# Eleven pages of the second sequence are issued by GpSimd at the end of the mLSTM stage

## The chip, the cores and the metric

The kernel runs on one core of one Trainium2 chip. The metric is the device time of one execution in microseconds, lower is better. The engines are TensorE (PE in the profile), its weight load (PEld), VectorE (DVE), ScalarE (ACT), GpSimd (POOL) and SyncE (SP). A "q" behind a name (POOLq) is that engine's sequencer.

## The reference

One decoder layer (DEPTH is 1) is computed for a prompt of 1024 tokens and for 8 sample sequences of 4 tokens with 4096 past tokens each. The mixer has an mLSTM branch and a sparse attention branch. For the change two parts matter:

```python
# mlstm_mixer: chunkwise recurrence, then per-head norm and output gate
h, C, n, m = mlstm_chunked(q, k, vh, i_pre, log_f, C0, n0, m0)
h = h * lax.rsqrt(jnp.mean(h * h, axis=-1, keepdims=True) + EPS) * p['m_norm']
h = jax.nn.sigmoid(og) * h.reshape(B, T, M_DIM)
# nsa_mixer: the past rows come through a page table; blocks of 32 rows are compressed
past = cache_nsa_kv[l][page_table].reshape(bs, past_len, 4, N_KV, N_HD)
blk = kb.reshape(B, nc, CMP_BLK, G, D) + pe[None, None, :, None, :]
flat = jnp.moveaxis(blk, 3, 2).reshape(B, nc, G, CMP_BLK * D)
kcmp = jax.nn.gelu(flat @ w1) @ w2        # and the same for the values
```

A sample sequence has 32 pages of 128 tokens. The compression reads the first two of the four parts of each page, which is 128 KB a page and 4 MB a sequence.

## The kernel before, in words

The kernel is a row of stages, each a block with one instruction stream per engine. The helper `stage` (line 135 on) opens and closes a stage: at its end every engine drains and all engines meet, and no engine starts on the next stage before the last of them has arrived. The profile puts these closing instructions (DRAIN, EVENT_SEMAPHORE) on line 146.

**The stage `mlstm` (line 515 on)** computes the prompt's mLSTM in 8 chunks of 128 tokens. Its streams are written out by hand. At its end PE turns the eight scaled output chunks (line 762), ACT copies them out of PSUM (line 816), and DVE closes with one memset that waits for all eight copies. GpSimd's last work there is the scaling of chunks 0 to 2 (line 628, `scale(i)`). SP meanwhile issues the 32 pages of the first sample sequence (sequence 0) into the buffer `first_pages` (line 565), in slots whose former content has been read by then, and then stores the prompt's final state (lines 598 to 600).

**The stage `sab` (`states_and_blocks`, line 1016 on)** computes the compressed blocks of the 8 sample sequences and their mLSTM step. The page buffers are two, used in turn: `first_pages` (called `kv`) and, right behind it, `sab_kv` (`kv1`); sequence n uses buffer n % 2. `load(eng, n, first, count, done)` (line 1088) reads page numbers from the table and issues one DMA a page (line 1093). For sequence 1, which goes into `sab_kv`, SP issues pages 0 to 15 and GpSimd pages 16 to 31, at the very start of the stage. For sequences 2 to 7, SP issues 12 pages, ACT 8 and GpSimd 12, and these wait until PE is through with both products of sequence n-2, the last user of the same buffer (`layer1_ready >= 2 * (n - 1)`). PE runs a fixed order: `queries_keys` (lines 1141 to 1144), `first(0, 0)`, `first(0, 1)`, two products on the prompt's own rows, `first(1, 0)`, `first(1, 1)`, and so on to `first(7, 1)`. `first(n, kv)` is the big product over the pages of sequence n (line 1001) and waits for their arrival.

In memory the second page buffer lies over tiles of the stage `mlstm`: its slots 0 to 15 (16 KB in each partition) over `kT`, which holds the numerators until the end of that stage, and slots 16 to 26 (11,264 bytes) over `xs`, `ys`, `mnorm`, `dec` and `kw` (11,648 bytes together).

Of the kernel before, what the change touches and what calls it, by code (L numbers as in the profile page):

```python
# [20 lines left out]
ds = bass.ds  # L21

P = 128
# [3 lines left out]
NTILE = TP // P  # L27
NSEQ, TS = 8, 4
# [12 lines left out]
PAST, PAGE = 4096, 128  # L41
NPAGE = PAST // PAGE
# [462 lines left out]


W1_AT = 221152


def heads_weights(ring):  # L510
# [4 lines left out]
def mlstm(nc, A, O, K, N, zm, zn, hm, cw, wqk, tokm, tokn, sm, pages, psum):  # L515
# [9 lines left out]
    with stage(nc, "mlstm") as (ctx, sem):  # L525
# [18 lines left out]
                 "ex_ready", "weights_ready", "mb_ready", "dec_ready", "exp_done", "score_ready", "weighted", "kw_ready", "update_ready",  # L544
                 "inter_ready", "intra_ready", "C_ready", "num_ready", "ss_ready", "tail", "square_ready", "root_ready",
                 "intra_copied", "gated", "factors_ready", "scaled", "scaled_pool", "scaled_act", "state_copied", "turned", "h_stored", "C_turned", "finished",
                 "stored")
        S = {n: sem(n) for n in names}
        block = ctx.enter_context(nc.Block())
        wide = lambda bank: psum[:, bank:bank + 2, :].rearrange("p b (h t) -> p (b h) t", h=2)[:, :, 0:MD + 1]  # L550
# [24 lines left out]
        def pages_over_queries(eng, some, done):  # L575
            page = page_numbers(nc, eng, pages, some[0], len(some), N["n_pool"])
            eng.wait_ge(S["inter_ready"], NTILE)
            for e, g in zip(some, page):
                first_page(eng, e, g, done)

        @block.sync
        def _(sp):
            sp.dma_start(xs[:, :, :, 0:3], A["m_state"]).then_inc(S["loaded"], 16)
            sp.dma_start(mnorm[:, :, :], A["m_norm"].partition_broadcast(P)).then_inc(S["loaded"], 16)
            sp.dma_start(O["p_mconv"], zm[:, :, TP - 3:TP]).then_inc(S["conv_kept"], 16)
            sp.dma_start(N["w1"][:, :, :, :], A["cmp_w1"]).then_inc(N["w1_ahead"], 16)
            sp.wait_ge(S["staged"], 4)
            sp.dma_start(O["s_mconv"], xs[:, :, :, TS:TS + 3]).then_inc(S["stored"], 16)
            sp.wait_ge(S["conv_kept"], 16)
            sp.dma_start(N["C"][:, :, :, :], A["s_C0"]).then_inc(N["C_ahead"], 16)  # L590
            sp.dma_start(O["zkv"], zn[:, 4:8, :]).then_inc(S["stored"], 16)
            sp.dma_start(O["tkv"], tokn[:, :, 0:2 * P]).then_inc(S["stored"], 16)
            sp.dma_start(O["winp"], A["winp"]).then_inc(S["stored"], 16)
            pages_over_keys(sp, N["kv_ahead"])
            pages_over_queries(sp, range(0, NPAGE // 2), N["kv_ahead"])
            sp.wait_ge(S["finished"], 1)
            sp.wait_ge(S["state_copied"], 1)
            sp.dma_start(O["p_C"], Ct[:, :, :]).then_inc(S["stored"], 16)
            sp.dma_start(O["p_n"], cn[:, :]).then_inc(S["stored"], 16)
            sp.dma_start(O["p_m"], mc[0:1, NTILE, :]).then_inc(S["stored"], 16)  # L600
            sp.wait_ge(S["stored"], 112)

        @block.gpsimd
        def _(pool):
            ones = tokm[:, 0:NTILE, C_V:C_V + MH * (MD + 1)].rearrange("p t (h v) -> p t h v", h=MH)[:, :, :, MD]
            nc.gpsimd.memset(ones, 1.0).then_inc(S["ones_set"], 1)
            pool.wait_ge(S["loaded"], 32)

            def weigh_keys(i):
                pool.wait_ge(S["weights_ready"], 1)  # L610
                pool.wait_ge(S["kt_copied"], 2 * MH)
                if i >= 2:
                    pool.wait_ge(S["update_ready"], i - 1)
                w = chunks(ex[:, WL, :])[:, i, :].unsqueeze(2).to_broadcast([P, MH, MD])
                nc.gpsimd.tensor_tensor(kw[:, i % 2, :, :], kt[:, i, :, :], w, ALU.mult).then_inc(S["kw_ready"], 1)

            def scale_output_gate(t):
                x = tokm[:, t, C_OG:C_OG + 512]
                nc.gpsimd.tensor_tensor(x, x, mnorm[:, :, :].rearrange("p h v -> p (h v)"), ALU.mult).then_inc(S["og_scaled"], 1)

            def gate(i):
                pool.wait_ge(S["og_scaled"], i + 1)
                pool.wait_ge(S["ss_ready"], i + 1)
                nc.gpsimd.tensor_tensor(chunk(num, i), chunk(num, i), tokm[:, i, C_OG:C_OG + 512].rearrange("p (h v) -> p h v", h=MH), ALU.mult
                                        ).then_inc(S["gated"], 1)

            def scale(i):
                nc.gpsimd.tensor_tensor(chunk(num, i), chunk(num, i), chunks(fac[:, :])[:, i, :].unsqueeze(2).to_broadcast([P, MH, MD]), ALU.mult
                                        ).then_inc(S["scaled_pool"], 1)

            weigh_keys(0)
            for i in range(1, NTILE):
                weigh_keys(i)
                scale_output_gate(i - 1)
                if i >= 3:
                    gate(i - 3)
            scale_output_gate(NTILE - 1)
            gate(NTILE - 3)
            gate(NTILE - 2)
            pool.wait_ge(S["factors_ready"], 1)  # L640
            for i in POOL_SCALES:
                pool.wait_ge(S["gated"], i + 1)
                scale(i)

        @block.tensor
        def _(pe):
# [369 lines left out]
def states_and_blocks(nc, A, O, K, N, zn, hm, tokm, sm, pages, ring, tile_at, spare, psum):  # L1016
# [7 lines left out]
    layer1_bank = lambda n, kv: 4 + kv if n == 1 else kv  # L1024
    with stage(nc, "sab") as (ctx, sem):
        assert nc.sbuf_base == N["kv_at"]
        top = N["kv_at"] + 4 * NPAGE * 2 * PAGE

        def sb(n, shape):
            nonlocal top  # L1030
# [1 line left out]
            top += -(-4 * int(np.prod(shape[1:])) // 32) * 32  # L1032
            return t

        kv_in = [N["kv"], sb("kv1", [P, NPAGE, 2 * PAGE])]
        NPR = TP // 2
        place, limit = spare

# [42 lines left out]
        per_head = lambda v, n: v.unsqueeze(2).to_broadcast([NS, MH, n])  # L1081
        per_all = lambda v: v.unsqueeze(1).to_broadcast([NS, MH, NS])
        SP_N, POOL_N, ACT_N = 12, 12, 8
        FIRST_SP = NPAGE // 2
        hard = lambda n: FIRST_SP if n == 1 else SP_N + ACT_N
        soft = lambda n: NPAGE - hard(n)

        def load(eng, n, first, count, done):
            page = page_numbers(nc, eng, pages, n * NPAGE + first, count, N["n_pool"])
# [14 lines left out]

        @block.sync
        def _(sp):
            load(sp, 1, 0, FIRST_SP, loaded)
            sp.dma_start(w2[:, :, :], A["cmp_w2"]).then_inc(S["w_loaded"], 16)
            sp.dma_start(rel[:, :], A["rel"]).then_inc(S["vec_loaded"], 16)
            sp.wait_ge(S["qk_ready"], 1)  # L1110
# [18 lines left out]

        @block.gpsimd  # L1130
        def _(pool):
            load(pool, 1, FIRST_SP, NPAGE - FIRST_SP, loaded_soft)
            for n in range(2, NSEQ):
                load(pool, n, SP_N + ACT_N, POOL_N, loaded_soft)

        @block.tensor
        def _(pe):
# [38 lines left out]
            def first(n, kv):  # L1176
# [3 lines left out]
                elif kv == 0:  # L1180
                    pe.wait_ge(loaded[n % 2], 16 * pages_before(n, hard))
                    pe.wait_ge(loaded_soft[n % 2], 16 * pages_before(n, soft))
                if n == 1 and kv == 0:
                    pe.wait_ge(S["qk_copied"], 3)
                elif n == 1:
                    pe.wait_ge(S["q_read"], 1)
                elif n == 2:
                    pe.wait_ge(S["act_ready"], kv + 1)
                elif n:
                    pe.wait_ge(S["act_ready"], 2 * (n - 1) + kv + 1)  # L1190
# [2560 lines left out]
def build(nc, A, O):  # L3751
    with ExitStack() as ctx:
# [20 lines left out]
        x = low  # L3773
# [15 lines left out]
        with ExitStack() as c:  # L3789
            N = {"n_pool": A["pool"].shape[0],  # L3790

                 "soft": {n: ctx.enter_context(nc.semaphore(n)) for n in ("c0", "c1", "n0", "n1")}}
            N.update({n: ctx.enter_context(nc.semaphore(n)) for n in ("w1_ahead", "C_ahead", "kv_ahead")})
            tile_at = lambda name, shape, at: nc.alloc_sbuf_tensor_at(name, shape, F32, offset=at)
            N.update(kv_at=nc.sbuf_base, kv=tile_at("first_pages", [P, NPAGE, 2 * PAGE], nc.sbuf_base),
                     w1=tile_at("block_w1", [P, 2, CB // 2, HD], W1_AT), C=tile_at("sample_C", [P, NSEQ, MH, MD], place["low"] + 4 * 4 * T))
            mlstm(nc, A, O, K, N, zm, zn, hm, cw, heads_weights(ring), tokm, tokn, sm, pages, psum)
            N.update(block_views(tile_at("blocks", [P, BLOCKS_W], place["tokm"])))
# [211 lines left out]
```

## Time and profile before

| | us |
|---|---|
| median of 3 runs | 2373.71 |
| lowest and highest of them | 2369.65, 2380.47 |
| the profiled execution, device time | 2377.2 |
| its span, first to last instruction | 2375.5 |
| PE busy in it | 2251.5 (95%) |
| GpSimd busy in it | 439.4 (18%) |
| granted TensorE clock, mean | 0.971 |

The span starts with the first instruction; all places in time below are microseconds from there. The stage `mlstm` ends at about 382.5 and the stage `sab` at about 498. A line of the profile names the engine, the source line, the operation, what is written and what is read, and the count; in brackets stands for how long the engine was idle before it and what released it.

### The profile page before, as it was taken

Reading aid. Unit: us, or ns where it says so; the run is one execution under the profiler, and the core shown is the slowest. Engines: PE = TensorE matmul, PEld = TensorE weight load, DVE = VectorE, ACT = ScalarE, POOL = GpSimd, SP = SyncE. Lnnn points to the kernel's source line nnn. Section 1 sums busy time; section 2 is a strip of 40 time slices with the busy share of each in tenths; the row PEclk is TensorE's granted clock in tenths of the full one; section 3 lists DMA queues with packets and bytes.
Section 4 is the critical chain, followed back from the end, with each engine's and each line's share of the span. In section 5 each row is a group of like instructions: output and inputs, shape, how many; then the busy total and the mean of one; then the engine's idle time right before and its main releaser. Section 6 shows DMA issues by size and latency. Waiting matters only on the chain. (4 is left out here: it accounts for less than half of the span.)

```text
span 2375.5 us, 39417 instructions
## 1 busy us (share of the span) xinstructions
PE 2251.5 (95%) x16031; PEld 2072.3 (87%) x16031; DVE 1083.8 (46%) x2432; ACT 719.8 (30%) x1444; POOL 439.4 (18%) x393
## 2 busy tenths in 40 slices
PE   8999998988988989999999999999999999999996
PEld 7799977856555689999999978999999999999995
DVE  2213354356666741222254346186545555542336
ACT  4221253135655630111342225352111111121123
POOL 0000035402223121121111100112222222122220
PEclk9999999879999999999999999999999999999998
DMA  4211097964434331210411444121111111111312
GB/s 146 97 49 46 27 187 242 308 224 124 144 126 150 115 113 41 69 43 27 153 36 45 160 173 162 43 91 63 45 45 45 46 53 45 35 43 47 118 41 82
DMA packets 114159, 228.71 MB, mean 96 GB/s; under 512 B 23394, under 2 KB 76291, under 8 KB 110588
## 3 DMA queue, kind: packets, MB, share of 16 engines
q1 hardware_dynamic: 91578, 182.12, 24.3%
q0 software_dynamic: 10368, 28.33, 3.6%
q10 hardware_dynamic: 12034, 15.76, 2.0%
q8 instruction: 127, 2.08, 0.4%
q14 instruction: 52, 0.43, 0.1%
HBM read 202.91 MB, written 27.45 MB: 97 GB/s over the span
## 5 line engine op out<-in xcount | busy, mean ns | idle before, releaser
L88 PE MATMUL psum<-x_half_high,ff_half 128*128 128x352 f32 x3240 | 789.4, 323 | 9.8 <-POOL ff_half L69 4.9
L88 PEld LDWEIGHTS psum<-x_half_high,ff_half 128*128 128x128 f32 x3240 | 566.3, 189 | 11.3 <-POOL ff_half L69 5.9
L88 PE MATMUL psum<-h_again_low,ff_half 128*128 128x352 f32 x1176 | 378.4, 322 | 0.0
L69 POOL TENSOR_TENSOR ff_half<-ring,ff_half 128x1024 fp32r<-128x1024 f32 (+2 forms) x85 | 177.4, 2087 | 751.2 <-ACT ff_half L3293 751.2
L88 PEld LDWEIGHTS psum<-h_again_low,ff_half 128*128 128x128 f32 x1176 | 222.2, 189 | 0.0
L3293 ACT ACTIVATE ff_half<-ring 128x1024 fp32r<-128x1024 f32 (+2 forms) x88 | 78.0, 888 | 428.7 <-PE psum L88 407.5
L88 PE MATMUL psum<-merged_high,oq_half 128*128 128x352 f32 x768 | 189.8, 327 | 9.3 <-DVE oq_half L69 7.7
L88 PE MATMUL psum<-mid_low,ff_half 128*128 128x352 f32 x516 | 166.3, 322 | 0.0
L88 PEld LDWEIGHTS psum<-merged_high,oq_half 128*128 128x128 f32 x768 | 136.1, 191 | 9.9 <-DVE oq_half L69 8.0
L88 PE MATMUL psum<-x_half_high,mg_w_high 128*128 128x352 f32 x384 | 124.0, 323 | 1.2 <-ACT gated L2317 1.2
L88 PE MATMUL psum<-h_again_low,mg_w_high 128*128 128x352 f32 x384 | 123.1, 321 | 0.0
L88 PE MATMUL psum<-x_half_high,mg_w_low 128*128 128x352 f32 x384 | 123.1, 320 | 0.0
L1945 ACT ACTIVATE na_pt<-psum 128x512 f32<-128x512 f32 (+1 forms) x170 | 86.4, 543 | 87.1 <-PE psum L1820 78.6
L1643 POOL DMA_DIRECT2D na_kv<-in_pool x128 | 69.2, 540 | 225.1 <-PE psum L1847 150.8
L1820 PEld LDWEIGHTS psum<-consts,na_p 128*128 128x128 f32 x528 | 57.8, 144 | 53.5 <-DVE na_p L2094 31.7
L3604 DVE TENSOR_TENSOR h_again<-h_again,psum 128x352 f32<-128x352 f32 x96 | 49.8, 520 | 117.3 <-PE psum L88 117.1
L88 PE MATMUL psum<-in_half,h_high 128*128 128x512 f32 (+3 forms) x360 | 102.7, 371 | 0.0
L1925 ACT ACTIVATE na_p<-na_p,na_nm 128x640 f32<-128x640 f32 (+7 forms) x128 | 92.8, 727 | 25.4 <-DVE na_nm L1961 25.2
L88 PEld LDWEIGHTS psum<-mid_low,ff_half 128*128 128x128 f32 x516 | 97.5, 189 | 0.0
L3572 DVE TENSOR_TENSOR ff_cv<-ff_cv,ff_row 128x352 f32<-128x352 f32 x66 | 68.8, 1042 | 56.1 <-ACT ff_cv L3339 56.1
L69 POOL TENSOR_TENSOR mg_w_low<-mg_w,mg_w_high 128x1536 fp32r<-128x1536 f32 x15 | 54.0, 3602 | 202.6 <-DVE mg_w_high L65 196.8
L1820 PE MATMUL psum<-consts,na_p 128*128 128x128 f32 x528 | 81.3, 289 | 9.4 <-DVE na_p L2094 7.6
(585 smaller groups left out, 4337.8 us busy)
## 6 DMA issues: line engine op xcount, KB each, us to landing
na_kv<-in_pool SPq DMA_DIRECT2D x128, 128.0 KB, 3.5
na_kv<-in_pool POOLq DMA_DIRECT2D x128, 128.0 KB, 4.0
mg_w<-in_w_merge SPq DMA_DIRECT2D x15, 768.0 KB, 4.4
ring<-in_f_wu SPq DMA_DIRECT2D x22, 512.0 KB, 3.6
ring<-in_f_wg SPq DMA_DIRECT2D x22, 512.0 KB, 3.6
first_pages<-in_pool SPq DMA_DIRECT2D x68, 128.0 KB, 6.2
x_kv<-in_mem_k SPq DMA_DIRECT2D x8, 1024.0 KB, 9.2
x_kv<-in_mem_v SPq DMA_DIRECT2D x8, 1024.0 KB, 8.6
```

The source lines that it names most:

```text
L69: return engine.tensor_tensor(low, x, high.bitcast(F32), ALU.subtract)
L88: ins = nc.tensor.matmul(out, w[a], x[b], start=first and n == 0, stop=last and n == 2)
L1643: eng.dma_start(kv[m % 2][:, b, 2 * PAGE * p:2 * PAGE * (p + 1)], A["pool"][ds(g, 1), :, 2 * PAGE:4 * PAGE].rearrange("a p x -> (a p) x")) ...
L1820: last = nc.tensor.transpose(out[:, c:c + P], src, K["ident"][:, :])
L1925: ins = nc.scalar.activation(x, x, ACT.Exp, bias=nm[:, b, g, i:i + 1], scale=-1.0, accum_out=sums[:, b, g:g + 1])
L1945: nc.scalar.activation(dst, psum[:, 4 + n % 2, 0:2 * m * P], ACT.Copy).then_inc(S["copied"], 1)
L3293: nc.scalar.activation(half(u)[:, 0, 0:n], ring[:, u % 2, 0:n], ACT.Copy).then_inc(S["w_high"], 1)
L3572: nc.vector.tensor_tensor(c, c, row[:, g, :], ALU.mult).then_inc(S["factored"], 1)
L3604: ins = nc.vector.tensor_tensor(z[:, f, col(g)], z[:, f, col(g)], bank(v), ALU.add)
```

## The change

GpSimd gets a new last piece of work in the stage `mlstm`: it reads 11 page numbers, waits on four semaphores and issues pages 16 to 26 of sequence 1 into the second page buffer, with a semaphore of their own (`kv1_ahead`). PE waits for that semaphore before `first(1, 0)`. In the stage `sab` SP then issues pages 0 to 11 of that sequence (it was 0 to 15) and GpSimd pages 12 to 15 and 27 to 31 (it was 16 to 31). The store of the sample's convolution state gets its own semaphore (`conv_stored`), since the new pages overwrite `xs`.

```diff
+SECOND_AHEAD = range(16, 27)
...
+        def second_sequence_ahead(eng):
+            page = page_numbers(nc, eng, pages, NPAGE + SECOND_AHEAD[0], len(SECOND_AHEAD), N["n_pool"])
+            eng.wait_ge(S["conv_stored"], 16)
+            eng.wait_ge(S["conv_ready"], 1)
+            eng.wait_ge(S["og_scaled"], NTILE)
+            eng.wait_ge(S["inter_ready"], NTILE)
+            for e, g in zip(SECOND_AHEAD, page):
+                eng.dma_start(N["kv1"][:, e, :], A["pool"][ds(g, 1), :, 0:2 * PAGE].rearrange("a p x -> (a p) x")).then_inc(N["kv1_ahead"], 16)
...
-            sp.dma_start(O["s_mconv"], xs[:, :, :, TS:TS + 3]).then_inc(S["stored"], 16)
+            sp.dma_start(O["s_mconv"], xs[:, :, :, TS:TS + 3]).then_inc(S["conv_stored"], 16)
...
-            sp.wait_ge(S["stored"], 112)
+            sp.wait_ge(S["stored"], 96)
+            sp.wait_ge(S["conv_stored"], 16)
...
             for i in POOL_SCALES:
                 pool.wait_ge(S["gated"], i + 1)
                 scale(i)
+            second_sequence_ahead(pool)
...
-        kv_in = [N["kv"], sb("kv1", [P, NPAGE, 2 * PAGE])]
+        kv_in = [N["kv"], N["kv1"]]
...
-        FIRST_SP = NPAGE // 2
-        hard = lambda n: FIRST_SP if n == 1 else SP_N + ACT_N
-        soft = lambda n: NPAGE - hard(n)
+        LOW, HIGH = SECOND_AHEAD[0], SECOND_AHEAD[-1] + 1
+        hard = lambda n: SP_N if n == 1 else SP_N + ACT_N
+        soft = lambda n: LOW - SP_N + NPAGE - HIGH if n == 1 else POOL_N
...
-            load(sp, 1, 0, FIRST_SP, loaded)
+            load(sp, 1, 0, SP_N, loaded)
...
-            load(pool, 1, FIRST_SP, NPAGE - FIRST_SP, loaded_soft)
+            load(pool, 1, SP_N, LOW - SP_N, loaded_soft)
+            load(pool, 1, HIGH, NPAGE - HIGH, loaded_soft)
...
                 if n == 1 and kv == 0:
+                    pe.wait_ge(N["kv1_ahead"], 16 * len(SECOND_AHEAD))
                     pe.wait_ge(S["qk_copied"], 3)
```

## Rows read from the trace of the kernel before

**Rows 1.** The page: span, busy time by engine.

```profile
span 2375.5 us, 39417 instructions
...
PE 2251.5 (95%) x16031; PEld 2072.3 (87%) x16031; DVE 1083.8 (46%) x2432; ACT 719.8 (30%) x1444; POOL 439.4 (18%) x393
```

**Rows 2.** Timeline of PE, 377 to 403: start, us, work, [idle <-releaser].

```profile
377.82 3.59 PE L762 MATMUL psum<-consts,kT 128*128 128x128 f32 x16 [0.63 <-ACT low L816]
382.72 0.38 PE L1141 MATMUL psum<-low,ring 128*128 128x32 f32 x2 [1.30 <-PEq L146]
...
389.11 8.34 PE L1001 MATMUL psum<-first_pages,block_w 128*64 128x128 f32 x128
...
402.84 3.71 PE L1001 MATMUL psum<-sab_kv,block_w 128*64 128x128 f32 x64
```

**Rows 3.** Waits of PE, 384 to 485, first and last of four: total, times, longest.

```profile
PE psum L1200 <- DVE blocks L1379: 0.7, 1, 0.7
...
PE psum L1171 <- issue: 0.5, 1, 0.5
```

**Rows 4.** Timeline of PE, 402 to 490.

```profile
414.95 5.38 PE L1001 MATMUL psum<-first_pages,block_w 128*64 128x128 f32 x64
...
485.83 4.54 PE L1001 MATMUL psum<-sab_kv,block_w 128*64 128x128 f32 x40 [3.43 <-DMA sab_kv<-in_pool]
```

**Rows 5.** Timeline of GpSimd, 370 to 396.

```profile
372.07 3.04 POOL L628 TENSOR_TENSOR kT<-kT,fac 128x512 f32<-128x512 f32 x3 [1.96 <-DVE fac L948]
384.67 0.71 POOL L1093 DMA_DIRECT2D sab_kv<-in_pool  x1 [9.56 <-issue]
385.61 8.71 POOL L1093 DMA_DIRECT2D sab_kv<-in_pool  x15 [0.23 <-issue]
```

**Rows 6.** Line 146 in 374:385: count, duration ns, first and last start.

```profile
L146 POOLq EVENT_SEMAPHORE  x2: 17/17/17, 382.5 to 382.6; - x2
L146 POOLq DRAIN  x1: 3137/3137/3137, 372.0 to 372.0; - x1
...
L146 DVEq DRAIN  x1: 19/19/19, 382.4 to 382.4; - x1
```

**Rows 7.** GpSimd's table read at the start of `sab`.

```profile
L106 POOLq TENSOR_LOAD <-pages x1: 1269/1269/1269, 382.6 to 382.6; - x1
```

**Rows 8.** GpSimd's pages in `sab`, 383 to 396.

```profile
L1093 POOL DMA_DIRECT2D sab_kv<-in_pool x16: 538/538/714, 384.7 to 393.8; - x16
...
DMA to landing us min/median/max: 4.2/5.7/7.6
```

**Rows 9.** GpSimd's last pages in the attention stage, 795 to 802.

```profile
L1643 POOL DMA_DIRECT2D na_kv<-in_pool x8: 538/538/538, 796.7 to 800.9; - x8
...
DMA to landing us min/median/max: 2.8/4.0/4.9
```

**Rows 10.** Line 146, 795 to 812; PE, same window; line 146, 476 to 500.

```profile
L146 POOLq DRAIN  x1: 5603/5603/5603, 800.8 to 800.8; - x1
...
805.82 1.06 PE L1766 MATMUL psum<-na_kv,na_qf 128*32 128x512 f32 x8 [1.84 <-DMA na_kv<-in_pool]
...
L146 POOLq DRAIN  x1: 11042/11042/11042, 476.6 to 476.6; - x1
```

**Rows 11.** SP's last 16 pages of sequence 0, 366 to 378.

```profile
L565 SPq DMA_DIRECT2D first_pages<-in_pool x16: 332/333/333, 368.8 to 376.6; - x16
...
DMA to landing us min/median/max: 2.1/2.4/2.9
```

**Rows 12.** By stretch: PE, PEld, DVE, ACT, POOL busy; PEclk, DMA share, GB/s.

```profile
380.00:384.00 4.00, 2.70 (x17) 2.14 (x15) 1.26 (x6) 1.59 (x3) 0.00 (x0) 0.85 0.02 4
384.00:391.00 7.00, 7.00 (x42) 5.54 (x43) 0.70 (x2) 3.49 (x7) 5.70 (x11) 0.55 0.78 213
391.00:411.00 20.00, 20.00 (x388) 18.26 (x384) 3.36 (x15) 3.09 (x8) 9.55 (x18) 0.99 1.07 340
```

**Rows 13.** The same, 416:418, inside `first(2, 0)`.

```profile
416.00:418.00 2.00, 2.00 (x22) 2.00 (x20) 0.00 (x0) 1.14 (x2) 1.82 (x5) 0.50 1.03 331
```

More of the change, by code:

```diff
@@ L546, in mlstm @@
                  "intra_copied", "gated", "factors_ready", "scaled", "scaled_pool", "scaled_act", "state_copied", "turned", "h_stored", "C_turned", "finished",
-                 "stored")
+                 "stored", "conv_stored")
         S = {n: sem(n) for n in names}
@@ L1026, in states_and_blocks @@
         assert nc.sbuf_base == N["kv_at"]
-        top = N["kv_at"] + 4 * NPAGE * 2 * PAGE
+        top = N["kv_at"] + 2 * 4 * NPAGE * 2 * PAGE
         def sb(n, shape):
@@ L3792, in build @@
                  "soft": {n: ctx.enter_context(nc.semaphore(n)) for n in ("c0", "c1", "n0", "n1")}}
-            N.update({n: ctx.enter_context(nc.semaphore(n)) for n in ("w1_ahead", "C_ahead", "kv_ahead")})
+            N.update({n: ctx.enter_context(nc.semaphore(n)) for n in ("w1_ahead", "C_ahead", "kv_ahead", "kv1_ahead")})
             tile_at = lambda name, shape, at: nc.alloc_sbuf_tensor_at(name, shape, F32, offset=at)
             N.update(kv_at=nc.sbuf_base, kv=tile_at("first_pages", [P, NPAGE, 2 * PAGE], nc.sbuf_base),
+                     kv1=tile_at("sab_kv", [P, NPAGE, 2 * PAGE], nc.sbuf_base + 4 * NPAGE * 2 * PAGE),
                      w1=tile_at("block_w1", [P, 2, CB // 2, HD], W1_AT), C=tile_at("sample_C", [P, NSEQ, MH, MD], place["low"] + 4 * 4 * T))
```

## The prediction

> **What bounds the kernel now.** I read the page first: PE is busy 2251.5 us of a span of 2375.5 us, 95% [rows 1]. So a change in page transfers can only show where PE stands still for them, or where it makes the stages meet later. The change touches two stretches, the end of the mLSTM stage and the stage `sab` behind it, so I read PE's timeline there. PE ends its last turn of the output chunks at 377.82 + 3.59 = 381.41, stands 1.30 us until the stages have met, starts `queries_keys` at 382.72, `first(0, 0)` at 389.11 and `first(1, 0)`, which reads the pages in question, at 402.84. That last row has no bracket: PE did not stand still for these pages [rows 2]. The waits of PE between 384 and 485 say the same over the whole stage: four waits, 0.7 + 0.6 + 0.5 + 0.5 = 2.3 us, on DVE, ACT and issue, none on a DMA [rows 3]. The first and only wait for pages is at 485.83, 3.43 us before `first(7, 0)` [rows 4]. Those are pages of sequence 7, and their issue waits for PE to finish sequence 5, six products after anything that the change moves.
>
> Then the meeting of the engines. GpSimd is idle from the end of its last scaling, 372.07 + 3.04 = 375.11, to its first page at 384.67 [rows 5]. Its closing DRAIN started at 372.0 and ended at 375.1. DVE's started last, at 382.4, and GpSimd's signals went out at 382.5 and 382.6 [rows 6]. So GpSimd has 382.5 - 375.1 = 7.4 us of slack, and the change puts its new work exactly there.
>
> **What the change removes in `sab`.** GpSimd issues 9 pages in place of 16 and SP 12 in place of 16. An issue on GpSimd takes 0.58 us from one to the next (0.94 us for the first, then 8.71 / 15), so 7 of them free it 4.1 us earlier [rows 5]. 11 pages of 128 KB, 1.44 MB, less are moved there; at the 340 GB/s of that stretch this is 4.2 us of DMA time [rows 12]. Value: nothing. Before, the last page was issued at 393.8 and pages took 4.2 to 7.6 us from issue to landing, so they were there by 401.4 at the latest, 1.4 us ahead of PE at 402.84 [rows 2, 8]. After it they are there some 4 us sooner, and PE is no sooner. The pages of sequence 2 also find emptier DMA engines, and PE didn't wait for them either [rows 3]. All later issues hang on PE's products. The earlier issue of `w2`, `rel` and `onehot` on SP is as idle a gain, for no wait of PE is on them. The second table read that GpSimd does now costs it at most the 1.27 us of the first one [rows 7], hidden by the same 1.4 us and more.
>
> **What it adds in the mLSTM tail, step by step.** (a) The table read, 1.27 us [rows 7]. The sequencer had passed all three scalings by 372.0, when it took up the DRAIN [rows 6], so I take it that the read goes on beside them, 372.0 to 373.3, and costs nothing; if it had to wait for them, it adds 1.3. (b) The four waits name things that the stage has finished by 375; they release at once. (c) Eleven issues behind the scalings. The first starts at about 375.2, the second 0.94 later, the others at 0.58: the last starts at 375.2 + 0.94 + 9 x 0.58 = 381.4 and ends at 381.9 [rows 5]. By itself that fits into the slack, 0.6 us ahead of 382.5.
>
> (d) The DRAIN behind them. This is the step on which the sum turns. At the end of the attention stage the last of eight page issues on GpSimd started at 800.9 and took 0.54, yet the DRAIN that stood behind it lasted from 800.8 to 806.4. PE, which waited for those pages, started at 805.82 [rows 9, 10]. At the end of `sab` the DRAIN behind the last pages lasted 11.04 us, from 476.6 to 487.6, and PE started on these pages at 485.83 [rows 4, 10]. So after page issues GpSimd's DRAIN ends when the data are there, 0.6 and 1.8 us after PE saw them, and not when the issue is done. Before the change GpSimd had no DMA in the mLSTM stage, so its DRAIN cost nothing; now the whole meeting waits for the pages to land. That is no wait in the program's text: it is behind GpSimd's DRAIN that PE, ACT, DVE and SP all stand.
>
> (e) How long the last page takes to land. In a quiet stretch SP's pages took 2.1 to 2.9 us with issues to 376.6 [rows 11]. GpSimd's eight took 2.8 to 4.9, median 4.0, beside SP's issues [rows 9], and 5.7 in the full stretch [rows 8]. SP's last pages of sequence 0 are through by about 379.5 (376.6 + 2.9), and between 380 and 384 the DMA engines have nothing (share 0.02) [rows 12], so I leave out the full stretch and take 4.0. The bounds are 2.1 and 4.9. The Trainium skill ("DMA: Bandwidth & Descriptors", section "Anatomy of one DMA") gives 2.0 us and the bytes at 436 GB/s for a DMA from GpSimd, for 128 KB an estimate of 2.3 us, and by that page the delay below would be some 1.9 us. No GpSimd row here is as short as that, and the measured median decides.
>
> The sum: 381.4 + 4.0 + 0.7 = 386.1, against 382.5, which is 3.6 us later for every engine. The low end is 381.4 + 2.1 + 0.6 - 382.5 = 1.6 us, the high end with the table read in line 381.4 + 1.3 + 4.9 + 1.8 - 382.5 = 6.9 us. SP's stores of the final state share the engines with the pages and land perhaps 1 us later than before, still ahead of 386.
>
> **What is late next.** PE leaves the meeting 3.6 us later and runs its fixed order. Nothing in the stage gives that back, since each later page issue moves with PE, and so does the wait of 3.43 us for sequence 7. One thing may move by a little: the granted clock. It is 0.55 between 384 and 391 and 0.99 after that [rows 12], behind a tail in which PE had little to do. With a longer pause the slow stretch may begin earlier or end later. I give it 0 +- 1 us.
>
> Against its own execution the sum is 2377.2 + 3.6 = 2380.8 us. The three runs have a median of 2373.7, 3.5 below that execution, so the predicted time is 2373.7 + 3.6 = 2377.3 us, 0.15% more. The runs themselves lie between 2369.65 and 2380.47, and about 0.5% (12 us) is what a measurement of this kernel can tell from no change, so I call this the same.
>
> **The rivals.** *The DRAIN costs nothing* (chance 0.2). The landing might be seen sooner in a quiet stretch, or the DRAIN might wait for something else that was late in both rows. Then the last issue, over at 381.9, is ahead of 382.5 and the time is 2373.7. Against it stand two rows out of two.
>
> *The relief reaches the late pages* (0.06). With 4.2 us less DMA work in `sab`, the wait for sequence 7 might shrink. All of it would be 3.43 us [rows 4], so without the delay 2370.3 us. Against it: the issues for sequences 3 to 7 start at PE's products, and 60 us lie between.
>
> *Everything is late together* (0.08). GpSimd's table read stands behind the scalings, and the last page lands as in the full stretch, at 7.6 us [rows 8]. That is 381.4 + 1.3 + 7.6 + 1.8 - 382.5 = 9.6 us, or 2383.3.
>
> *The clock stays down* (0.03), the one that ends slower beyond doubt. PE's pause before `queries_keys` grows from 1.3 to 5 us. If the lower level (1.2 GHz, 0.5 in the rows) then held not until 391 but until 411, its 388 matmuls of these 20 us would go at the 11 a us that PE does at 0.50 [rows 13], not at 19.4 [rows 12]: 35 us in place of 20, so 15 us more and 3.6 for the delay, 2392 us. It decides from about 12 us, which is a low clock until some 406. Against it: the clock was back at 391, within 2 us of the start of the dense product at 389.11 [rows 2], and the same dense product follows here.
>
> *The change does not do what it says*: the pages would have to be issued after the meeting all the same. The four waits are on work that is over by 375, so I give this nothing of its own.
>
> **How the numbers follow.** The forecast, 1.6 to 6.9 us later, has 0.63. Its own range is 2375.3 to 2380.6. The median of a few runs can fall some 3 us off that on either side (the three shown span 10.8 us), and the case without cost and the case of everything late must be let in: 2370.5 to 2383.5. Faster by over 0.5% (below 2361.8) is in none of the cases, 0.02 for what I have not seen. Slower by over 0.5% (above 2385.6) takes the clock's case and a piece of the one before, 0.05. The rest, 0.93, is the same.
>
> **What would show it.** In the changed profile GpSimd has eleven page issues from about 375.2, the last starting near 381.4. A start near 376.5 would show the table read in line. GpSimd's DRAIN on line 146 ends near 386 and the signals follow within 0.1 us, in place of 382.5; PE's bracket before line 1141 reads about 5 us in place of 1.30. From there PE's rows stand as before, 3.6 us later: `first(1, 0)` near 406.4 without a bracket, and the wait before `first(7, 0)` again near 3.4 us. The prediction is wrong if the signals of line 146 go out by 383, if PE stands still anywhere before `first(7, 0)` for a DMA, or if the wait for sequence 7 changes by more than 1 us.

## The result, and the profile after

The changed kernel takes 2383.01 us (median of 20 runs, 2372.59 to 2387.84), the kernel before 2376.61 (20 runs, 2369.65 to 2381.18). The ratio is 1.0020 with a 95% interval of 1.0011 to 1.0028, which is 2.6 to 6.7 us more. The forecast was 2377.3, with 3.6 us more as its core, in a range of 2370.5 to 2383.5: the time lies just inside the upper end of that range and within 0.5% of before, as expected, and the cost is larger than its core.

The page after (profiled execution: 2383.68 us) answers to [rows 1]: the span is 6.5 us longer.

```profile
span 2382.0 us, 39422 instructions
...
PE 2253.7 (95%) x16031; PEld 2074.4 (87%) x16031; DVE 1083.6 (45%) x2432; ACT 719.5 (30%) x1444; POOL 441.1 (19%) x397
```

The timeline of PE after the change, to be laid beside [rows 2, 4]:

```profile
374.21 1.56 PE L774 MATMUL psum<-consts,kT 128*128 128x128 f32 x12 [1.13 <-POOL kT L639]
378.77 3.39 PE L774 MATMUL psum<-consts,kT 128*128 128x128 f32 x16 [0.63 <-ACT low L828]
387.40 0.60 PE L1154 MATMUL psum<-low,ring 128*128 128x32 f32 x2 [5.23 <-PEq L146]
395.31 9.25 PE L1013 MATMUL psum<-first_pages,block_w 128*64 128x128 f32 x128
409.78 3.71 PE L1013 MATMUL psum<-sab_kv,block_w 128*64 128x128 f32 x64
418.23 5.39 PE L1233 MATMUL psum<-sab_qT,sample_C 128*128 128x4 f32 x32
493.96 5.92 PE L1013 MATMUL psum<-sab_kv,block_w 128*64 128x128 f32 x64 [3.33 <-DMA sab_kv<-in_pool]
506.19 1.98 PE L1789 MATMUL psum<-blocks,zn 64*128 64x32 f32 x32 [0.85 <-PEq L146]
```

Three rows of the kernel before are needed beside it that the prediction did not use, from the same view: the first turned chunk of the tail, the products with the state, and the first product of the stage behind `sab`.

```profile
373.26 1.56 PE L762 MATMUL psum<-consts,kT 128*128 128x128 f32 x12 [1.14 <-POOL kT L628]
411.29 3.73 PE L1219 MATMUL psum<-sab_qT,sample_C 128*128 128x4 f32 x32
498.10 1.98 PE L1775 MATMUL psum<-blocks,zn 64*128 64x32 f32 x32 [0.85 <-PEq L146]
```

The 6.5 us divide as follows. The changed profile comes to the tail 374.21 - 373.26 = 0.95 us later, before anything of the change runs. From there to the next stage it takes 506.19 - 374.21 = 131.98 us against 498.10 - 373.26 = 124.84, so 7.1 more. Behind that it gives 1.6 us back, where the program is the same. The 7.1 us, by PE's rows:

- the pause at the meeting, 5.23 against 1.30: +3.9;
- from the first product of `sab` to `first(1, 0)`, 409.78 - 387.40 = 22.38 against 402.84 - 382.72 = 20.12: +2.3;
- from `first(1, 0)` to the next stage, 506.19 - 409.78 = 96.41 against 498.10 - 402.84 = 95.26: +1.2, in which the products with the state alone went from 3.73 to 5.39 us;
- the turns of the tail, 0.2 shorter.

The meeting first. GpSimd's timeline, then the lines of its page issues:

```profile
373.02 3.04 POOL L639 TENSOR_TENSOR kT<-kT,fac 128x512 f32<-128x512 f32 x3 [1.95 <-DVE fac L960]
376.00 6.12 POOL L589 DMA_DIRECT2D sab_kv<-in_pool  x11
388.32 2.33 POOL L1105 DMA_DIRECT2D sab_kv<-in_pool  x4 [6.19 <-issue]
```

```profile
L589 POOLq MOVE sab_kv<-in_pool x11: 29/29/29, 374.7 to 381.1; - x11
L589 POOL DMA_DIRECT2D sab_kv<-in_pool x11: 536/536/711, 376.0 to 381.6; - x11
...
DMA to landing us min/median/max: 4.0/4.9/5.4
```

Line 146 in the changed kernel, 374 to 395, answers to [rows 6]:

```profile
L146 POOLq EVENT_SEMAPHORE  x2: 17/17/17, 387.2 to 387.2; - x2
...
L146 POOLq DRAIN  x1: 5547/5547/5547, 381.6 to 381.6; - x1
...
L146 DVEq DRAIN  x1: 19/19/19, 383.2 to 383.2; - x1
L146 SPq COMPARE_BRANCH  x1: 38/38/38, 384.8 to 384.8; - x1
```

GpSimd's DRAIN began at 381.6 and ended 5.5 us later, at 387.1. DVE was ready at 383.2, so GpSimd held the others for 3.9 us. But SP too is late: it reached line 146 at 384.8. Before, it was there at 380.5. SP's waits say why, first of the kernel before, then of the changed one (waits of SP around the meeting: total, times, longest):

```profile
SPq L146 <- DMA out_p_m<-mc: 1.8, 1, 1.8
```

```profile
SPq L146 <- DMA out_p_m<-mc: 5.3, 1, 5.3
```

SP waited 3.5 us longer for its last small store. It had issued that store at 378.3 before and at 379.1 now, so from issue to the end of the wait it is 2.2 us before and 5.7 after. SP's last page of sequence 0 is slow too: issued at 377.5, it took 5.9 us to land, against 2.9 at most before [rows 11]. SP did not decide here (384.8 against 387.1), but it is a second door, and it would have held the meeting beyond DVE's 383.2 by itself.

By stretch, after the change, to be laid beside [rows 12]: the DMA engines, which had nothing between 380 and 384, are full there, and the granted clock is 0.79 between 391 and 411 in place of 0.99.

```profile
380.00:384.00 4.00, 2.16 (x11) 1.76 (x9) 0.61 (x2) 2.28 (x5) 2.02 (x4) 0.69 0.99 344
384.00:391.00 7.00, 3.60 (x16) 2.93 (x16) 1.89 (x6) 0.00 (x0) 2.33 (x4) 0.63 0.40 102
391.00:411.00 20.00, 20.00 (x310) 18.03 (x310) 3.36 (x15) 5.43 (x12) 8.03 (x15) 0.79 0.73 225
```

Cut to the stretches in which the lower level (0.50, that is 1.2 GHz) held throughout, it is 385 to 391 in the kernel before (the level changed back at 391.5) and 386 to 399 after (back at 399.5):

```profile
385.00:391.00 6.00, 6.00 (x35) 4.83 (x36) 0.00 (x0) 3.49 (x7) 5.37 (x11) 0.50 0.87 245
```

```profile
386.00:399.00 13.00, 11.60 (x68) 9.56 (x69) 1.89 (x6) 3.49 (x7) 5.01 (x9) 0.50 0.74 221
```

### The profile page after: what moved, and what is told of

Read it like the earlier page. It is cut to its first block and busy times, and to the rows that moved or that the text cites. A ratio compares the mean times of both kernels' runs of the same rounds, so it can differ in the third digit from the quotient of the medians.

```text
span 2382.0 us, 39422 instructions
## 1 busy us (share of the span) xinstructions
PE 2253.7 (95%) x16031; PEld 2074.4 (87%) x16031; DVE 1083.6 (45%) x2432; ACT 719.5 (30%) x1444; POOL 441.1 (19%) x397
```

## The experiments

All are timed in five rounds beside the kernel before on the same chip. Apart from the ratio, each is read by PE's marks in its one profile, all worked out as above. *Pause*: PE's idle time at the meeting. *Small*: from the first product of `sab` to the start of `first(0, 0)`. *Dense*: the duration of `first(0, 0)`, 128 matmuls. *Way*: from the first product of `sab` to `first(1, 0)`; small and dense are part of it. *Rest*: from `first(1, 0)` to the next stage. *Total*: from the first turned chunk to the next stage. There is one profile for each kernel, so a mark says what happened in that execution.

```
kernel        pause  small  dense    way   rest   total   ratio [95%]
before         1.30   6.39   8.34  20.12  95.26  124.84
changed        5.23   7.91   9.25  22.38  96.41  131.98   1.0020 [1.0011, 1.0028]
after_again    4.71   7.92   9.25  22.39  96.42  131.64   1.0026 [1.0011, 1.0041]
pool6          3.28   7.91   8.20  21.33  94.52  127.09   0.9993 [0.9978, 1.0007]
pool3          2.33   7.91   9.28  22.35  96.35  128.81   0.9999 [0.9986, 1.0011]
pool1_late     3.46   7.92   8.10  21.21  95.06  127.67   1.0004 [0.9990, 1.0017]
sp4            1.30   6.43   8.30  19.92  94.71  124.05   1.0007 [0.9990, 1.0024]
pause          1.30   7.91   9.53  22.67  96.47  135.14   1.0051 [1.0031, 1.0071]
no_pages       1.30   7.91   8.68  21.83  93.31  125.22   0.9997 [0.9980, 1.0013]
warm_after     1.64   7.20   9.10  21.48  92.49  126.97   1.0016 [1.0001, 1.0031]
warm_ahead     1.01   4.44   7.21  16.84  97.24  127.40   1.0009 [0.9995, 1.0022]
warm_before    0.59   4.43   7.21  26.24  93.56  128.40   1.0021 [1.0009, 1.0032]
warm_gate      1.05   4.43   7.21  18.84 102.87  130.78   1.0027 [1.0013, 1.0041]
warm_gate_sp   1.19   5.74   9.08  20.02  99.26  128.49   1.0012 [0.9997, 1.0027]
```

**What the meeting waits for: pool6, pool1_late, sp4.** The first kernel issues 6 pages ahead, so that GpSimd is done early.

```diff
-SECOND_AHEAD = range(16, 27)
+SECOND_AHEAD = range(16, 22)
```

> The changed kernel with 6 pages ahead on GpSimd in place of 11. In the changed kernel the issues are 0.56 us apart, and GpSimd's DRAIN ended 5.5 us after the last issue had started. Theory (the DRAIN waits until the pages have landed): the last issue starts 2.8 us sooner, so the stages meet 2.8 us sooner, and PE's pause before the first product of the next stage is 5.2 - 2.8 = 2.4 us; the time lies about 0.1% above the kernel before. Rival 1 (only the issue time counts): the issues are over 3 us before PE's last turn, the pause is 1.3 us as before and the time is that of before. Rival 2 (the relief of the DMA engines is worth something): faster than before.

It took 2375.47 us against 2376.97. Its pages, line 146 and SP's wait:

```profile
L589 POOL DMA_DIRECT2D sab_kv<-in_pool x6: 536/538/711, 375.0 to 377.8; - x6
...
DMA to landing us min/median/max: 3.4/4.3/6.0
```

```profile
L146 POOLq DRAIN  x1: 6980/6980/6980, 377.1 to 377.1; - x1
...
L146 SPq COMPARE_BRANCH  x1: 38/38/38, 383.7 to 383.7; - x1
```

```profile
SPq L146 <- DMA out_p_m<-mc: 5.1, 1, 5.1
```

The last issue starts at 377.8 and is over by 378.4, and the DRAIN still lasts until 384.1. The slowest landing, 6.0 us from the last issue, would be 383.8. So the DRAIN goes by the landing and not by the issues. The meeting is at 384.2 and was at 387.2; 1.0 us of that is the earlier tail of this profile (first turned chunk at 373.2 against 374.2). So five pages fewer moved it 2.0 us and not the 2.8 expected, since the last page now took 6.0 us to land. It is still 2 us behind DVE (382.1).

The second puts one page, issued just ahead of the old meeting, in place of eleven.

```diff
-SECOND_AHEAD = range(16, 27)
+SECOND_AHEAD = range(16, 17)
...
             eng.wait_ge(S["inter_ready"], NTILE)
+            eng.wait_ge(S["turned"], NTILE - 1)
```

> One single page ahead on GpSimd, issued only when PE has turned the seventh of the eight output chunks. Theory (landing): the issue starts about 0.3 us after that turn, and DVE's close comes 1.5 us later; landing takes 2.8 to 4.9 us and the DRAIN 0.7 more, so PE's pause before the first product of the next stage is 3.4 to 5.5 us, as long as with eleven pages. Rival (the amount of traffic makes the delay): one page is 0.4 us of DMA time, so the pause is at most 1.9 us. Rival (issue time): 1.3 us.

It took 2377.67 against 2376.97. PE's timeline at the meeting, GpSimd's DRAIN, and the landing of that page:

```profile
384.77 0.60 PE L1155 MATMUL psum<-low,ring 128*128 128x32 f32 x2 [3.46 <-PEq L146]
```

```profile
L146 POOLq DRAIN  x1: 2557/2557/2557, 381.6 to 381.6; - x1
```

```profile
L590 POOL DMA_DIRECT2D sab_kv<-in_pool x1: 712/712/712, 381.6 to 381.6; - x1
...
DMA to landing us min/median/max: 2.4/2.4/2.4
```

One page is enough: landed at 384.0, DRAIN over at 384.1 or 384.2. The third lets SP issue four pages behind its three stores, and GpSimd none.

```diff
             sp.dma_start(O["p_m"], mc[0:1, NTILE, :]).then_inc(S["stored"], 16)
+            second_sequence_ahead(sp)
...
-            second_sequence_ahead(pool)
```

> Four pages ahead, issued by SP after the three stores of the final state, none by GpSimd. The last is issued at about the time of PE's last turn. Theory (only GpSimd's DRAIN waits for landing): PE's pause stays at 1.3 to 1.8 us although the pages are still on their way when the stages meet, and the time is that of before. Rival (any page in flight holds up the meeting): the pause is 3 us or more.

It took 2378.61 against 2376.97. PE at the meeting, SP's page issues, and SP's wait for the store:

```profile
383.18 0.38 PE L1154 MATMUL psum<-low,ring 128*128 128x32 f32 x2 [1.30 <-PEq L146]
```

```profile
L589 SPq DMA_DIRECT2D sab_kv<-in_pool x4: 333/342/382, 379.7 to 381.3; - x4
...
DMA to landing us min/median/max: 2.4/2.5/2.8
```

```profile
SPq L146 <- DMA out_p_m<-mc: 0.3, 1, 0.3
```

The first page lands at 382.1 at the earliest and the last at 383.7 at the earliest, while the meeting was over at 382.9 and the pause is 1.30 as before. So it is pages issued by GpSimd that hold the meeting, not pages in flight. And with the delay gone, four pages ahead bring nothing that the timing shows (0.9990 to 1.0024).

**Only three pages: pool3.** With three, GpSimd's DRAIN should be over before DVE is ready.

```diff
-SECOND_AHEAD = range(16, 27)
+SECOND_AHEAD = range(16, 19)
```

> The changed kernel with 3 pages ahead on GpSimd in place of 11. With six, the last issue started 3.4 us ahead of PE's last turn and its page landed 2.7 us behind it; three end 1.7 us sooner and are half the data. Theory (the meeting waits for the landing, so what lands within the slack is free): GpSimd's DRAIN ends before DVE's close, PE's pause is 1.3 to 1.8 us, its way to the product on sequence 1 is 20.1 us, and the time is that of before. Rival (any page issue on GpSimd ahead of the meeting costs at least one full landing): the pause is 3 us or more.

It took 2378.57 against 2377.22. Its pages landed within 4.7 us of issues that ended at 377.2, and the DRAIN (376.4 + 5.75 = 382.1) is out of the way, but the pause is not back at 1.3. PE's timeline, then line 146 with SP's wait:

```profile
384.30 0.60 PE L1154 MATMUL psum<-low,ring 128*128 128x32 f32 x2 [2.33 <-PEq L146]
```

```profile
L146 DVEq DRAIN  x1: 19/19/19, 383.0 to 383.0; - x1
L146 SPq COMPARE_BRANCH  x1: 38/38/38, 383.9 to 383.9; - x1
```

```profile
SPq L146 <- DMA out_p_m<-mc: 3.2, 1, 3.2
```

Here the second door decides: DVE was ready at 383.0, SP at 383.9, and the signals went out at 384.1. That is 0.9 to 1.0 us of pause that no DRAIN of GpSimd explains, and the way, 22.35 us where 20.1 was expected, is that of the changed kernel.

Whether the three pages made SP late is not shown. SP issued its last store at 380.2, 1.9 us later than before: 0.9 is the late tail of this profile, and the issue of the first store took 1.6 us in place of 0.75. From there to the end of the wait it is 3.6 us. That is more than the 2.2 before, but without any page of GpSimd in flight the same store took 2.7 to 3.7 us in pool1_late and in four kernels that come below (`pause`, warm_before, no_pages and warm_gate). SP's wait in no_pages, a kernel whose GpSimd issues nothing there:

```profile
SPq L146 <- DMA out_p_m<-mc: 3.0, 1, 3.0
```

With six and eleven pages it is 5.5 (pool6), 4.8 (after_again) and 5.7 us (changed), beyond all of these. The profiled execution of pool3 is also the longest of its twelve (2387.69 us, the median is 2378.57).

**The changed kernel again, its pages taken out, its pause filled: after_again, no_pages, warm_after.** The first repeats the changed kernel on the chip of the other two.

> The changed kernel once more, for a second trace and as the neighbour of the next run. If the slow stretch behind the meeting belongs to the pause, PE's pause is again about 5.2 us and PE again takes about 22.4 us from the first product of the next stage to the first one on sequence 1 (before: 20.1). If it was a chance draw, that stretch is nearer to 20.1 us.

It took 2382.13 against 2375.82, and its marks are those of the first profile: way 22.39 and rest 96.42 against 22.38 and 96.41. The second clears the eleven slots in place of loading them, so it leaves these pages out of the result.

```diff
-            for e, g in zip(SECOND_AHEAD, page):
-                eng.dma_start(N["kv1"][:, e, :], ...).then_inc(N["kv1_ahead"], 16)
+            nc.gpsimd.memset(N["kv1"][:, SECOND_AHEAD[0]:SECOND_AHEAD[-1] + 1, :], 0.0
+                             ).then_inc(N["kv1_ahead"], 1)
```

> The changed kernel in which pages 16 to 26 of sequence 1 are not loaded at all: GpSimd clears their slots at the end of the mLSTM stage in place of issuing them, so the compression of that sequence computes on zeros there. This gives the whole relief of the next stage without any DMA behind GpSimd. Theory (the relief is worth nothing, the cost is all in the landing): PE's pause is 1.3 us, its way from the first product to the one on sequence 1 is 20.1 us, from there to the next stage 95 us, and the time is that of before. Rival (the relief is worth something): from the product on sequence 1 to the next stage PE takes 92 us or less, and the time is 2 to 4 us below before.

It took 2374.81 against 2375.82 (0.9980 to 1.0013). It has the whole relief, 1.44 MB never moved in either place, and a pause of 1.30; its gain is not told from none. So the relief is worth at most 4.8 us (the lower end of the interval) and by the best estimate 0.7, and the cost of the changed kernel is gone with its pages. The wait for sequence 7 stayed at 3.6 us. Two marks missed what was expected: the way is 21.83 and not 20.1, and the rest 93.31 and not 95. The rest of the kernel before and of this one, as stretches:

```profile
402.84:498.10 95.26, 88.16 (x1101) 80.44 (x1099) 28.18 (x69) 15.51 (x38) 34.45 (x65) 0.87 0.90 292
404.80:498.11 93.31, 85.93 (x1102) 78.14 (x1099) 28.19 (x69) 15.21 (x38) 34.46 (x66) 0.91 0.90 296
```

PE stands still as long in both (95.26 - 88.16 = 7.1 us, 93.31 - 85.93 = 7.4), and its clock is 0.91 in place of 0.87. So the shorter rest is a faster clock and not a wait that the relief took away.

The third fills the pause with five products that nobody reads (the profile counts two matmuls for each).

```diff
                 last.then_inc(S["turned"], 1)
+            for _ in range(5):
+                nc.tensor.matmul(psum[:, 3, :], zn[:, 0, 0:P], zn[:, 0, 0:512], start=True, stop=True)
```

> The changed kernel with five more products of 128 by 512 on PE, into a PSUM bank that is dead by then, behind the last turned chunk: they fill PE's pause while GpSimd's DRAIN waits. The meeting stays where it is, about 5 us later than before. Theory (the pause lowers the clock of what follows): the stretch from the first product of the next stage to the first one on sequence 1 falls from 22.4 to 20.1 us or less, and the time is about 3 us below the changed kernel. Rival (the pages in flight, or chance, slow it): the stretch stays at 22.4 us and the time with it.

It took 2379.51 against 2375.82, and 2382.13 for the changed kernel on that chip. PE's timeline:

```profile
379.75 4.46 PE L777 MATMUL psum<-zn 128*128 128x512 f32 x10
385.85 0.38 PE L1156 MATMUL psum<-low,ring 128*128 128x32 f32 x2 [1.64 <-PEq L146]
```

The meeting is as late as in after_again (the signals at 385.6 in both), yet the total is 4.7 us shorter. The timed gain, 2.6 us, is not settled: the two intervals overlap. In the profiles nothing of it comes ahead of `sab` (385.85 - 372.85 = 13.0 us from the first turned chunk, against 12.8); 0.9 is on the way and 3.9 in the rest. The granted clock still fell, at 386.7, and rose at 397.0. The expected way of 20.1 was missed (21.48), so five products did not keep the clock up.

**A busy GpSimd without pages: pause.** Ten products of GpSimd on buffers that nobody reads any more were to delay the meeting without any DMA.

```diff
                 scale(i)
+            pool.wait_ge(S["inter_ready"], NTILE)
+            for i in range(10):
+                nc.gpsimd.tensor_tensor(kw[:, 0, :, :], kw[:, 1, :, :], kw[:, 1, :, :],
+                                        ALU.mult).then_inc(S["busy"], 1)
+                pool.wait_ge(S["busy"], i + 1)
```

> The kernel before with no page moved, and ten more products on GpSimd at the end of the mLSTM stage, on two buffers that are dead by then (about 1.1 us each), so that the stages meet about as late as in the changed kernel. Theory (the pause of PE lowers the granted clock of what follows): the pause is 4 to 5.5 us, and from the first product of the next stage to the first product on sequence 1 PE takes 22.4 us as in the changed kernel, against 20.1 before; the time is 4 to 7 us over before. Rival (the pages in flight slow what follows, or the one trace was a chance draw): 20.1 us, and the time is 4 us over before.

It took 2387.15 against 2376.97 (six runs). The run is no clean pause: GpSimd was done at 387.9, but what came late was DVE. Its scalings of one chunk, in the kernel before and beside GpSimd's products:

```profile
377.87 1.14 DVE L967 SCALAR_TENSOR_TENSOR kT<-kT,fac,tokm 128x128 f32<-128x128 f32 x4
```

```profile
381.79 4.57 DVE L971 SCALAR_TENSOR_TENSOR kT<-kT,fac,tokm 128x128 f32<-128x128 f32 x4
```

PE waited in its turns and not at the meeting, and the granted clock was 0.50 from 378.5 to 402.4. The way is 22.67, like the changed kernel's, with no page in flight between 380 and 391. So the 2.3 us on the way do not need the pages; in this run a tail in which PE did little went with the same slow way.

**What a warm PE meets: warm_before, warm_ahead, warm_gate, warm_gate_sp.** If the clock costs that much, keeping it up should pay in either kernel. To the kernel before were added one filling product ahead of the first and the fourth turned chunk, one behind the last, and three ahead of `first(7, 0)`.

```diff
             for n, i in enumerate(OUT_ORDER):
+                if n in (0, 3):
+                    keep_warm()
...
                 last.then_inc(S["turned"], 1)
+            keep_warm()
...
+            for _ in range(3):
+                nc.tensor.matmul(psum[:, 3, :], zn[:, 0, 0:P], zn[:, 0, 0:512], start=True, stop=True)
             first(7, 0)
```

> The kernel before, no page moved, with filling products on PE where it stands still: one ahead of the first turned chunk, one ahead of the fourth, one behind the last, and three ahead of the product on sequence 7 where PE waits 3.4 us for pages. Theory (PE's standing still lowers the clock behind it): the stretch to the product on sequence 1 falls from 20.1 to 18 us, the first product on sequence 7 from 5.9 to 3.7 us, and the time is 3 to 5 us below before. Rival (the clock falls there anyway): the stretches stay, and the time is that of before or 1 us over it.

It took 2379.87 against 2375.82: slower. Clock 1.0 through the tail brought PE to `first(1, 0)` at 398.6, and there it stood, because now the pages of sequence 1 were late (SP's last one took 15.2 us to land):

```profile
407.49 5.13 PE L1007 MATMUL psum<-sab_kv,block_w 128*64 128x128 f32 x64 [8.88 <-DMA sab_kv<-in_pool]
```

The next kernel is the changed one with the same fill, six products behind the last chunk in place of one.

> The changed kernel with filling products on PE: one ahead of the first turned chunk, one ahead of the fourth, six behind the last, which fill the pause, and three ahead of the product on sequence 7. In the kernel before with such products PE came to the product on sequence 1 so early that it waited 8.9 us for its pages; here 11 of them are ahead. Theory (the pages ahead are worth something once PE is fast enough to need them): PE takes 17.5 us or less from the first product to the one on sequence 1 and waits 2 us at most for pages there, and the time is 2 to 5 us below the kernel before with filling products, which makes it about that of before. Rival (the pages ahead are worth nothing anyway): PE waits for pages there as long as without them.

It took 2380.15 against 2378.16. PE's timeline at `first(1, 0)`, and the clock from 380 to 414:

```profile
403.16 3.71 PE L1020 MATMUL psum<-sab_kv,block_w 128*64 128x128 f32 x64
```

```profile
380.00:414.00 34.00, 32.99 (x470) 26.95 (x468) 5.31 (x22) 7.75 (x17) 14.53 (x27) 1.00 0.86 270
```

Here the pages ahead pay: the wait of 8.9 us is gone, and the way is 16.84. But from the first turned chunk to the first product of `sab` it takes 13.3 us against 8.6 in warm_before, and the rest is 97.24 us against 93.56. The rest has one wait for pages, 2.0 us for sequence 6 (2.2 in warm_before); what differs is the clock, 0.88 against 0.91 over that stretch. The last two kernels hold back the issues for sequence 2 until sequence 1 has landed, on the kernel before and on sp4, both with the fill.

```diff
             if n >= 2:
                 eng.wait_ge(S["layer1_ready"], 2 * (n - 1))
+            if n == 2:
+                eng.wait_ge(loaded[1], 16 * hard(1))
+                eng.wait_ge(loaded_soft[1], 16 * soft(1))
```

> The kernel before, no page ahead, with the filling products (one ahead of the first and of the fourth turned chunk, one behind the last, three ahead of the product on sequence 7) and one wait more: the issues of the pages of sequence 2 wait until all 32 pages of sequence 1 have landed. Theory (the 8.9 us wait came from the pages of sequence 2 sharing the DMA engines with the last pages of sequence 1): those land by 397.5, PE waits 1 us at most for them, takes 17.5 us to them, and the time is 3 to 5 us below before. Rival (the pages of sequence 1 are late by themselves): PE waits as long as before, and the later issue for sequence 2 costs 1 to 3 us more.

> The same with four pages of sequence 1 issued ahead by SP behind its three stores, none by GpSimd. Theory: the pages of sequence 1 land 1.5 us earlier than without them, PE's way to them is the same or up to 1 us shorter, the meeting is not later by more than 0.5 us, and the time is 3 to 6 us below before. Rival (SP's extra issues hold up the meeting): the meeting is 1.5 us later and eats the gain.

They took 2383.77 and 2380.46 against 2378.16 (ratios 1.0027, 1.0013 to 1.0041, and 1.0012, 0.9997 to 1.0027). In warm_gate the wait for sequence 1 fell from 8.9 to 2.0 us, so most of it had come from the pages of sequence 2 moving beside them. But a wait for sequence 2 came in its place, as PE's timeline of warm_gate shows; in warm_gate_sp, where the clock fell in spite of the fill (dense 9.08), it is 6.6 us.

```profile
423.19 5.95 PE L1008 MATMUL psum<-first_pages,block_w 128*64 128x128 f32 x64 [8.47 <-DMA first_pages<-in_pool]
```

So in warm_before and warm_gate what the clock gained came back as waits for pages, which changed places, and in warm_ahead it was lost at the later meeting and in the rest. No kernel of this study beats the kernel before by more than its interval: pool6 (0.9993), no_pages (0.9997) and pool3 (0.9999) all reach over 1.

## Why the prediction was right, and where its sizes were off

**The relief in `sab` is worth nothing: right.** `first(1, 0)` has no bracket after either, PE has no wait for a DMA before `first(7, 0)`, and that wait is 3.33 us against 3.43 [rows 4]. The sharper test is no_pages: with 1.44 MB less and no delay the time is the same within 0.9980 to 1.0013. The margin was smaller than the prediction read, though. It took 401.4 as the last landing for sequence 1, from GpSimd's pages alone. SP's sixteen, in the kernel before, took up to 9.1 us:

```profile
L1093 SPq DMA_DIRECT2D sab_kv<-in_pool x16: 332/336/706, 384.1 to 393.1; - x16
...
DMA to landing us min/median/max: 2.2/5.2/9.1
```

The slowest is the last one, landed at 393.1 + 9.1 = 402.2, so the pages were 0.7 us ahead of PE and not 1.4. It holds only while PE is slow on the way there: warm_before turned the same pages into a wait of 8.9 us.

**Steps (a) to (c), table read, waits and issues: right.** GpSimd's sequencer was at the first page number at 374.7, while the scalings ran to 376.1, so the read was hidden. The last issue starts 381.6 - 376.06 = 5.5 us behind the end of the scalings, where 0.1 + 6.2 = 6.3 was worked out: the issues came at 0.53 to 0.58 us, and the first took 0.71 and not 0.94.

**Step (d), the DRAIN waits for the landing: right, and shown.** It ended 0.1 to 0.3 us behind the last landing in pool1_late, pool6 and pool3 (384.0 to 384.1, 383.8 to 384.1, 381.9 to 382.1) and 0.5 behind it in the changed kernel (386.6 to 387.1), closer than the 0.7 us allowed for. sp4, with pages in flight at the meeting and no pause, leaves only GpSimd's own DMAs as what the DRAIN waits for. The rival by which the DRAIN costs nothing fell with the first row of line 146.

**Step (e), the landing: at its upper bound.** It was 4.9 us for the median, 5.4 at most and 5.0 for the last page, on which the step turns, against 4.0 taken and 4.9 as the upper bound. The stretch was not quiet: the eleven pages filled it themselves (DMA share 0.99 between 380 and 384). The Trainium skill ("DMA: Bandwidth & Descriptors", section "Anatomy of one DMA") gives 2.0 us and the bytes at 436 GB/s, an estimate of 2.3 us here. The one page of pool1_late agrees with it, 2.4 us; the eleven do not. For the meeting the errors of (c), (d) and (e) nearly cancel, by luck: 3.6 us were expected and +3.9 measured.

**SP's stores: mis-sized, without effect in the changed kernel.** The prediction let them land "perhaps 1 us later"; SP was at line 146 4.3 us later (384.8 against 380.5), of which 0.95 is the late tail of this profile. It stayed ahead of GpSimd, as forecast. In pool3, where GpSimd is early, it decides. From its issue to the end of SP's wait the store took 2.2 to 3.7 us in the kernels without a page of GpSimd in flight and 4.8 to 5.7 with six or eleven. SP's own four pages in sp4 leave it at 3.6 (the short wait of 0.3 us there is only because SP came to it behind its four issues). Why GpSimd's pages slow it was not looked into.

**The granted clock, 0 +- 1 us: the term that was mis-sized.** Way and rest grew by 2.3 and 1.2 us in both profiles of the changed kernel. With this the sum is 3.9 + 2.3 + 1.2 - 0.2, some 7.1 us, in the profile, against 3.6 forecast and 6.9 as its high end, and the ratio's centre in the timed runs, 4.8 us, lies between. That the time fell into the range owes something to luck: the room above came from a table read in line and a slower landing, not from the clock, and the base of the forecast, the median of three runs (2373.7), was 2.9 us below that of all twenty (2376.6). The argument was that the same dense product brings the clock back as before. It does, but it starts after more slow work. In the kernel before the first small products still ran at the upper level: the first pair took 0.38 us [rows 2], and the clock fell at 384.6, two us into them. Small is 6.39 us there, 4.4 where the clock stays up (warm_before) and 7.91 in every run without a fill whose clock was down from the meeting on; that is 1.5 us of the 2.3. What is left is the dense product, 9.25 us against 8.34 and 7.21 warm: the clock rose 4.2 us after its start and not 2.4. In the rest the products with the state took 1.7 us more, as a longer low stretch fell on them (420.0 to 426.8 in place of 415.4 to 418.8), and 0.5 came back elsewhere.

What stays open is how much of this follows from the pause. Small is 6.4 us in two runs with a pause of 1.3 and 7.9 in all with more than 2. But no_pages has 7.91 with a pause of 1.30, because there the clock was down from 376.9 on. And dense does not follow the pause: 8.10 at 3.46 us, 9.28 at 2.33. So a part of the clock's price may be how its changes happen to fall on the program, and one profile for each kernel can't tell that from the pause. In the profiles with a late meeting way and rest together are 0.5 (pool6) to 3.4 us (changed) longer than before; a rule for it is not shown, and with a pause of 1.30 `pause` has 3.8 more as well.

**The rival of the clock that stays down** (2392 us) did happen in part: the lower level held until 399.5 and not 411. **Everything late together** did not: no table read in line, no landing of 7.6 us.

## What to carry to other kernels

Where stages meet behind a DRAIN, an idle GpSimd is not free for DMA issues: the meeting then waits until its data have landed, even for a single 128 KB page that is issued just ahead of it (3.5 us of pause against 1.3). Pages that are wanted early can go on SP's queue, behind its stores (sp4 kept the pause at 1.3). Before moving transfers ahead, look whether PE ever stands still for them; here it did not until its clock was kept up. And look at the pages of all queues: the last to land was SP's.

## What the runs showed of the hardware that was not expected

- GpSimd's DRAIN covers its own DMAs to their landing: 2.6 us behind one page, 5.5 us behind eleven, over 0.1 (one page), 0.2 (three), 0.3 (six) and 0.5 us (eleven) after the last landing. SP's DRAIN takes 7 ns with four of its pages in flight (sp4).
- While six or eleven of GpSimd's pages were being moved, SP's last small store was waited for 5.1 us (6) and 4.3 and 5.3 (11, two profiles). Without them it was 1.8 in the kernel before and up to 3.3 (warm_gate); the 3.2 us with three pages are not told from that.
- A product on GpSimd with both inputs in SBUF slowed DVE's scalings fourfold, 1.14 us to 4.57 for four. The Trainium skill ("SBUF — State Buffer", section "Who interferes with whom") says that a DVE instruction with two SBUF inputs contends with a GpSimd instruction that reads SBUF; the `pause` run agrees.
- The full clock through the tail was worth 2.0 us in the small products and 1.1 in the dense one (4.43 and 7.21 against 6.39 and 8.34), and more than that came back as a wait for pages.
